# Convolved projection from its ninth row tile on, and the projection back, in two-by-two blocks with seven products

## The reference

```python
FFN_HIDDEN = 2816        # 22 tiles of 128
FFN_CONV = 3

def causal_depthwise_conv(x, w, b):
    xp = jnp.pad(x, ((0, 0), (k_width - 1, 0), (0, 0)))
    y = b
    for k in range(k_width):
        y = y + w[k] * xp[:, k:k + seq]
    return y

def conv_ffn(x, w_in, conv_w, conv_b, w_out):
    h = causal_depthwise_conv(x @ w_in, conv_w, conv_b)     # [1024, 5632]
    val, gate = jnp.split(h, 2, axis=-1)
    return (jax.nn.silu(gate) * val) @ w_out                # [1024, 1024]

f = conv_ffn(rms_norm(x, norm_ffn_g), ffn_w_in, ffn_conv_w, ffn_conv_b, ffn_w_out)
x = x + f
```

## Time and profile before

| | |
|---|---|
| median of 3 runs | 2450.54 us |
| span of the profiled execution | 2450.4 us |
| TensorE busy | 2352.4 us (96%) |
| VectorE / ScalarE / GpSimd busy | 1305.0 / 1205.5 / 919.7 us |
| TensorE, 1950 to 2400 us | busy 450.0 of 450 us |
| DMA, mean over the span | 78 GB/s |

### The profile page before, as it was taken

How to read it: one execution, slowest core, us unless ns; L and a number is a source line. 1 busy time by engine, 2 the same in 40 slices (tenths; PEclk the granted TensorE clock), 3 DMA queues, 4 the chain that set the end, 5 groups by cost and what they waited for, 6 DMA issues and landing times.

```text
span 2450.4 us, 35232 instructions
## 1 busy us (share of the span) xinstructions
PE 2352.4 (96%) x12078; PEld 1996.2 (81%) x12078; DVE 1305.0 (53%) x2729; ACT 1205.5 (49%) x2873; POOL 919.7 (38%) x1133
## 2 busy tenths in 40 slices
PE   7999999999999999999999998989899999999999
PEld 6888787878888878888888887877678888888887
DVE  7444667667885333356656565687866213322331
ACT  6444556656775444456656565555544213322331
POOL 5554322311245642221122223677765322322321
PEclk9999999999999999999999999999999999999999
DMA  6322101111243332322222235322223111111112
GB/s 220 112 70 65 39 23 31 35 29 50 65 135 98 97 120 72 95 76 81 82 90 83 85 92 161 117 82 87 74 85 96 57 43 52 50 50 48 49 52 85
DMA packets 305985, 191.87 MB, mean 78 GB/s; under 512 B 63760, under 2 KB 284176, under 8 KB 305296
## 3 DMA queue, kind: packets, MB, share of 16 engines
q1 hardware_dynamic: 305808, 189.61, 26.2%
HBM read 170.16 MB, written 19.40 MB: 77 GB/s over the span
## 4 chain that ended last, share of the span: by engine, by line
PE 82%; DVE 5%; ACT 4%; issue 4%; POOL 4%; DMA 1%; SPq 0%; POOLq 0%; DVEq 0%; ACTq 0%
PE PS L1544 21%; PE PS L1546 21%; PE PS L1545 21%; PE PS L1690 5%; PE PS L1657 5%; PE PS L1644 3%; PE PS L1645 2%; POOL WS L2375 2%; ACT PY L1775 1%; PE PS L1699 1%; POOL HT L2434 1%; POOL PT L2375 1%; PE PS L1599 1%; DVE EO L2227 1%; PE PS L1681 1%
## 5 line engine op out<-in xcount | busy, mean ns | idle before, releaser
L2375 POOL TENSOR_TENSOR WS<-WR,WS 128x256 fp32r<-128x256 f32 x773 | 595.0, 788 | 1206.1 <-ACT WS L1775 1205.4
L1544 PE MATMUL PS<-HT,WS 128*128 128x512 f32 x1760 | 709.4, 403 | 32.4 <-POOL HT L2434 10.1
L1546 PE MATMUL PS<-HT,WS 128*128 128x512 f32 x1760 | 690.7, 392 | 0.0
L1545 PE MATMUL PS<-HT,WS 128*128 128x512 f32 x1760 | 689.1, 392 | 0.0
L1775 ACT ACTIVATE WS<-WR 128x256 fp32r<-128x256 f32 x788 | 295.2, 409 | 259.0 <-PE PS L1546 221.2
L1544 PEld LDWEIGHTS PS<-HT,WS 128*128 128x128 f32 x1760 | 332.8, 189 | 102.6 <-issue 15.1
L1546 PEld LDWEIGHTS PS<-HT,WS 128*128 128x128 f32 x1760 | 332.5, 189 | 72.4
L1545 PEld LDWEIGHTS PS<-HT,WS 128*128 128x128 f32 x1760 | 333.6, 190 | 62.6
L1775 ACT ACTIVATE PT<-PS 128x512 fp32r<-128x512 f32 x352 | 185.9, 529 | 225.5 <-PE PS L1657 225.2
L2002 DVE TENSOR_TENSOR PT<-PS,PT 128x512 fp32r<-128x512 f32 x352 | 210.9, 609 | 68.5 <-ACT PT L1775 66.2
L1690 PE MATMUL PS<-PT,QKV 128*128 128x256 f32 (+1 forms) x1248 | 209.3, 289 | 3.2 <-DVE YB L2181 2.3
(11 more groups left out here) (195 smaller groups left out, 3702.2 us busy)
## 6 DMA issues: line engine op xcount, KB each, us to landing
WR<-in_ffn_in SPq DMA_DIRECT2D x120, 256.0 KB, 2.9
WR<-in_w_in_odd SPq DMA_DIRECT2D x106, 256.0 KB, 3.0
EO<-in_grid SPq DMA_DIRECT2D x48, 384.0 KB, 3.1
WR<-in_w_in_even SPq DMA_DIRECT2D x100, 128.0 KB, 2.5
WR<-in_w_out_odd SPq DMA_DIRECT2D x48, 256.0 KB, 2.9
yd<-PY SPq DMA_DIRECT2D x44, 256.0 KB, 3.3
WR<-in_w_in_even SPq DMA_DIRECT2D x34, 256.0 KB, 2.9
WR<-in_w_out_even SPq DMA_DIRECT2D x64, 128.0 KB, 2.8
```

Of the source, the lines that this page charges most:

```text
L1544: e.matmul(out, wh, rh, start=start, stop=False)
L1545: e.matmul(out, wh, rl, start=False, stop=False)
L1546: return e.matmul(out, wl, rh, start=False, stop=stop)
L2375: e.tensor_tensor(ws(i, 1, n), RAW[raw_slot(u)][:, o:o + n], f32(ws(i, 0, n)), ALU.subtract).then_inc(s_wlop.sem, 1)
```

## The change

The 28 tiles "in" from the ninth row tile on, and the whole projection back, are done as two-by-two block products with seven products of half size for eight. A `Quad` is one such product: for "in" the value and gate tile j (two block rows), the two halves of the 1024 input features, and the two halves of the tokens; for "out" two output tiles, even and odd hidden tiles, and the two halves of the tokens. Two quads (x = 0, 1) run interleaved as a unit: 7 units "in" (numbers 0 to 6 here), then 6 units "out", two for each of the groups of 4, 4 and 3 pairs of hidden tiles. A unit is 14 products of 12 matmuls (9 in the last two units). Products 0, 2, 4, 6 of a quad add up in one bank, 3 and 5 in another.

Both sides need sums: of weights (`s1` to `s4`, each 128x512, "weight sum", two by POOL, two by DVE), of the normed input (`turn_sums`, 32 DVE instructions of 128x512 and 16 splits during the n=1 passes), and of the hidden tiles (`pair_sums`). The seven moving blocks of each pair of hidden tiles are stored to a new DRAM tensor `ud` (77 blocks of 256 KB) and fetched and split again ("u load", "u split") during the unit before their group begins: 28 splits in unit 6, 28 in unit 8, 21 in unit 10. `X` is spilled to DRAM ("x spill", 8 x 512 KB), its tiles serve as room for the "in" units, and are fetched back ("x reload") when unit 7 begins. Weights are split 8 products ahead, now 512 columns at a time. After each product a "post" copies (ACT) or adds (DVE) the bank to a half tile; the product four later writes the same bank and waits for that post. The splits "half hi" and "half lo" are gone; the n=0 passes store their result instead.

```diff
+Y_BANKS, X_BANKS, Z_BANKS = ((1, 3), (5, 7)), (4, 6), (2, 0)
+GROUPS = ((0, 4), (8, 4), (16, 3))
+SPLIT_OF = (A11, A12, A11, ADD, A21, A12, A22)
...
+        def turn_sums():
+            for k in range(4):
+                ...
+                put("turn raws", k, tmp, base, free)
+                put("turn sums", tmp, base)
+                for z, (b, i) in enumerate(((2, 3), (3, 0), (4, 1), (6, 2))):
+                    put("turn split", tmp[i], b, k, base, hi, turned[b, k])
...
-                p.hi = s_fa.add()
-                put("half hi", p, n)
-                put("half lo", p, n)
+                if n == 0:
+                    put("u store", [HBUF[p.buf]], u.i, STORED_AT[b], d_h[p.buf], [(s_fd, p.product)])
...
+        def weigh(p):
+            p.before = [lambda: (s_gm, p.no - n + 1)]
+            on = (s_glv, s_glv, s_glp, s_glp, s_glv, s_glp, s_glp)[i]
+            put("weights", p)
...
+            for t, p in enumerate(run):
+                put("product", p)
+                if t:
+                    post(run[t - 1])
+                if t + n - 1 < len(run):
+                    weigh(run[t + n - 1])
+                ...
+                        if 0 <= b < 7 and z // 2 == z2 and z < GROUPS[g][1]:
+                            split_hidden(g, b, z, s0 - 14 + 2 * b + 2)
+                if 14 * entered - 4 <= t:
+                    bring_back(t)
...
+                elif kind == "product":
+                    w.wait_ge(s_gh, p.no + 1)
+                    w.wait_ge(*p.lo)
+                    w.wait_ge(*until[p.bank])
+                    for k in range(m.n):
+                        w.wait_ge(*p.ready[k])
+                        ...
+                        e.matmul(out, wh, rh, start=p.first and k == 0, stop=False, skip_group_check=True)
+                        e.matmul(out, wh, rl, start=False, stop=False, skip_group_check=True)
+                        last = e.matmul(out, wl, rh, start=False, stop=k == m.n - 1, skip_group_check=True)
+                    until[p.bank] = p.post
...
+                elif kind == "x spill":
+                    w.wait_ge(s_nd, ffn[1].nd[7])
+                    e.dma_start(d["xs"][c, :, :], X[:, c, :]).then_inc(d_xt[c].sem, 16)
+                elif kind == "x reload":
+                    e.dma_start(X[:, c, :], d["xs"][c, :, :]).then_inc(d_xt[c].sem, 16)
```

More of the change, by code:

```diff
@@ L1391, in odd_last @@
                     pool_task(1, (4, 6, 8, 9).index(i))
-            for i in range(16):
+            for i in range(2 * PLAIN):
                 half_task(i // 2, HID * (i % 2), 1)
[L1394 to L1418, removed]
@@ L1420, in enter_in @@
-        def enter_in(j, base, g0, g1):
-            plan.append(Ffn("in", j, base, g0, g1, *add_units(in_units(d["ffn_in"], [(base + 128 * j, 128)]))))
+        units_of = [[Quad("in", PLAIN + 2 * u + x, None, u, x) for x in (0, 1)] for u in range((HT_TILES - PLAIN) // 2)]
+        for group in GROUPS:
+            for v in range(2):
+                units_of.append([Quad("out", 4 * v + 2 * x, group, len(units_of), x) for x in (0, 1)])
+        quads = [m for unit in units_of for m in unit]
+        run = [Product(m, i, 0) for unit in units_of for i in range(7) for m in unit]
@@ new lines, in start_products, with open_products @@
+        def start_products():
+            early = [(s_mm, state["mm"]), (s_acc, s_acc.n), (s_sums, s_sums.n), (s_pp, blocks[1, 7].lo)] + ffn[1].lo
+            late_ = [turned[b, k] for b in (2, 3, 4, 6) for k in (2, 3)]
+            rooms.extend((r, early if r < 4 else late_ + early) for r in range(len(ROOM)))
+            urooms.append((3, late_ + early))
+            take_rooms()
+            state["opened"] = open_products
+        def open_products():
+            if not places and at["split"] == len(subs):
+                order = sorted(range(5), key=lambda k: max(split_after(k)))
+                places.extend([(k, split_after(k)) for k in order] + [(k, None) for k in range(5, 9)])
+            while places and state.setdefault("split", 0) < 5 and all(i in used for i in places[state["split"]][1]):
+                weigh(run[state["split"]])
+                state["split"] += 1
@@ new lines, in take_rooms, with sum_of @@
+        def take_rooms():
+            while rooms and wanted:
+                m, which = wanted.pop(0)
+                r, after = rooms.pop(0)
+                m.raw[which] = r
+                if which == ADD:
+                    m.landed[which] = after
+                else:
+                    m.landed[which] = [(d_room[r], d_room[r].add(16))]
+                    put("weight load", m, which, r, lambda after=after: after)
+        def sum_of(m, name, on, out, a, b, op, need):
+            m.sums[name] = (on, on.add())
+            cut = slice(0, 128 * m.n)
+            put("weight sum", on, ROOM[m.raw[out]][:, cut], ROOM[m.raw[a]][:, cut], ROOM[m.raw[b]][:, cut], op, need)
@@ new lines, in centre, with go, taps @@
+        def centre(m, c, t, col, need, at_, then):
+            def go():
+                mid = (s_ga, s_ga.add())
+                put("centre", m, c, t, col, need + list(x_at.get(t, ())), )
+                soon(at_ + 1, lambda: taps(mid))
+            def taps(mid):
+                at1 = s_gd.add()
+                done_ = (s_gd, s_gd.add())
+                put("taps", m, c, t, col, at1, mid)
+                if c == CV[m.x]:
+                    m.val = done_
+                else:
+                    m.gate = done_
+                then()
+            soon(at_, go)
```

620 lines of the change are left out of this document (470 added, 150 removed).

## The result

The changed kernel takes 2435.76 us (median of 4 runs, 2434.73 to 2439.86) where the kernel before, on the same chip, takes 2449.72 (4 runs, 2446.56 to 2451.54): a ratio of 0.9948, 95% interval 0.9934 to 0.9962. It is faster by 14.0 us and not by the 45 of the forecast, and it lies 1.8 us outside the range. The profiled execution took 2434.73 us, its span is 2432.9.

A forecast was written before the change was run, and what follows sets the result against it. TensorE was taken to bound the kernel, busy 2352.4 of 2450.4 us. The terms -67.9 + 2 + 14 + 1 - 2 + 3 + 4 = -45.9 gave 2405 us, own range 2392 to 2428, overall range 2384 to 2434.

The forecast's parts named there:

- Products, -67.9: Both projections: 300 matmuls fewer at an unchanged 0.2265 us each save 67.9 us.
- Units "in", +2: First six units: VectorE and GpSimd demand 33.2 of 38.05 us together and fit; 2 us lost, 0 to 15.
- Unit 6 itself: 28 hidden-block splits overload VectorE and GpSimd by 13.4 to 17.4 us; posts may lag 8.2, so TensorE waits 5 to 9.
- Unit 7, "about 5 us more show": X tiles fetched back land 5.0 to 8.2 us after their last taps; first posts wait, costing about 5 us more.
- Units 8 and 10, +1: Hidden splits in unit 8 make common demand even with the unit, 1 us (0 to 8); unit 10 nothing.
- n=0 passes, -2: Dropping "half lo" and eight ScalarE splits shortens the chain before the 6.4 us pooling wait: -2 us, -6 to 0.
- Spill, +3: n=1 passes: the 4.2 MB spill of X in SP's queue delays the next weights, 3 us, 0 to 12.
- Turning, +4 (0 to 10): n=1 passes: 40 added VectorE instructions put it 12 to 20 us behind; four banks allow 16.3; 4 us lost.
- Clock: After a TensorE wait of some 4 us or more, the low clock adds about 2 us; counted at units 6 and 7.
- all hidden: Rival, chance 0.18: unit 6's lag is absorbed, since only posts are tight; -67 us, 2383 us.
- Whole durations: Rival, chance 0.15: two-operand VectorE and GpSimd instructions never overlap; units "in" 1.1 over, unit 6 24.5 over; 2420 us.
- VectorE waits out every GpSimd instruction: Rival, chance 0.08: VectorE's queue waits so, TensorE follows it wherever both sums exceed the unit; slower, 2477 us.

The follow-up runs named there:

- e9: Changed kernel with all instructions of the turned input 16 columns wide instead of 512 and the X spill spread over eight steps: 2416.19 us, ratio 0.9863.
- e13: e1 with 15 of GpSimd's 17 instructions in unit 6 cut to 16 columns, VectorE's queue unchanged: 2415.98 us, ratio 0.9859.
- e1: Changed kernel with the fetches of X tiles 0 and 2 one step earlier, ahead of that step's hidden-block loads in SP's queue: 2429.77 us, ratio 0.9916.
- e8: Changed kernel with all instructions of the turned input 16 columns wide instead of 512: 2419.97 us, ratio 0.9876.
- e4: Changed kernel with the eight X spills issued one per piece of work, weight loads between them, instead of all at once: 2434.85 us, ratio 0.9939.
- e5: Changed kernel with early reload, turning spread over more of the n=1 passes and spill spread, all three together: 2413.27 us, ratio 0.9850.

## Why the prediction was wrong, point by point

- **Products, -67.9.** Right: 543.8 to 475.7 us is -68.1, at an unchanged pace. A unit takes 38.08 us where 38.05 was said.
- **Units "in", +2.** 0 us in units 1 to 5, and 4.4 in unit 0; in the range, but not for the reason given. TensorE's wait of 2.8 us in unit 0 ended with ScalarE's first post. That stood behind a silu of the last pass, which waited 4.95 us for VectorE's taps, and VectorE had low parts and sums of weights ahead of these, some at 1.78 us each. It isn't the lateness of the opening: in e9, where that is gone, unit 0 takes 42.6. I had no term for the change from passes to products.
- **Unit 6 itself.** 5 to 9 us of waits and 2 of clock were said; it has 7.3 us of waits and is 9.9 us long over 38.08. That VectorE and GpSimd hold each other up is the cause, as e13 shows, and the price of 0.44 us that a VectorE instruction takes out of GpSimd's time was good (1.70 - 1.295 = 0.41). But the count was wrong: of the 28 low parts only 15 of VectorE and 4 of GpSimd ran in unit 6, 6 and 3 in unit 7. With 27 + 8 instructions of VectorE and 18 of GpSimd, as e13 has them in the unit, the same sum gives 27 x 0.44 + 8 x 0.98 + 18 x 1.295 = 43 us (an estimate), 5 over, which the allowance of 8.2 would have covered. So the 7.3 us agree by luck. A mean over the unit is also too coarse, since the low parts stand in its later part; what that alone costs no run shows.
- **Unit 7, "about 5 us more show".** This step failed. It cost 21.5 us: waits of 16.7, the rest low clock behind them. I took the reload to start when its tile's last tap ends, and to be alone in SP's queue. I had not laid the queue of SP beside VectorE's: the reloads stood behind loads that wait for late low parts, and the second one's stood behind the very post that waited for the first reload. e1 undoes that for 8.5 us. And unit 7 inherits VectorE's lateness (another 5.8, e13), while 8.2 us of allowance had been used up in unit 6; I counted it for both. The 14 us of both units were 31.4.
- **Units 8 and 10, +1.** The size is right by luck: both take 38.08, and 1.4 us are lost in unit 9.
- **n=0 passes, -2.** The direction was right: the long wait is 2.6 us shorter, the whole part 4.8, within my range (-6 to 0). That the missing low parts are the reason fits, but no run tests it.
- **Spill, +3.** In range (0 to 12): 4.3 without the turning (e9 against e8), 5.0 with it, where e4 also starts the turning later. But the issue of eight stores took SP 8.15 us, where I had taken the 4.15 of eight loads.
- **Turning, +4 (0 to 10).** This term failed too: 17.2 (e8). I compared VectorE's delay (12 to 20 us) with the 16.3 us that four banks give. The wait did not come by VectorE's lateness alone: high parts of the turned input stand in ScalarE's queue ahead of weight splits and centre taps, and ScalarE stood 6.62, 3.82, 2.02 and 8.14 us before them. I named who waits for VectorE at the banks, and not who is queued behind the waiting instruction on ScalarE. With the spill spread, spreading the turning gives 8.0 us back (e4 to e5) and leaving it out 16.4 (e4 to e9), so about half of its cost is its place in the queues; how the rest divides between the engines' own work and ScalarE's waits no run shows.
- **Clock.** I gave it 2 us, once. The products' stretch is 37.2 us longer than its matmuls and its waits are 27.6, so about 10 us are low clock there; in the opening, waits grew by some 17 us and the stretch by 22.6, so about another 5. I had also priced only waits of some 4 us and more: behind those of 3.83, 3.27 and 2.76 us the mean granted clock of the next 5 us was 0.50, 0.66 and 0.71.

The sum by what was measured: -67.9 + 4.4 + 31.4 + 1.4 - 4.8 + 22.6 = -12.9, and with the 4.4 us from upstream -17.3, where the two spans differ by 17.5.

The rivals: "all hidden" is out. "Whole durations" had the better time (2420) for a wrong reason: it charged six units "in" 1.1 us each, and they have 0. "VectorE waits out every GpSimd instruction" has the price of one instruction right. In unit 6 a VectorE instruction with SBUF operands takes up to 1.78 us, its own 0.69 and most of GpSimd's 1.295. But it is paid in full only while both queues are full, so TensorE loses nothing in units 1 to 5: VectorE works about 32 us in each, 7 more than alone, and still rests.

The Trainium skill ("SBUF — State Buffer", section "SBUF: two separate sides") calls the shared port an exclusive lock for the whole instruction. Its turn-taking agrees with the rule. By whole durations a pair would take 0.688 + 1.295 = 1.98 us; the trace has 1.70. Only part of the 0.28 us between them is overlap of the two engines, since each engine's own instructions overlap a little as recorded: in a row they start 0.60 us apart on VectorE and 1.25 on GpSimd, 1.85 together. Where rule and trace differ the trace decides: a pair costs 1.70.

What stays open: in e13 unit 7 is still 7.1 us over. TensorE waits 4.8 us there, 1.9 for ScalarE's weight splits and the rest for posts; what is behind these wasn't tested. More rooms weren't tried.

## What to carry to other kernels

When a transfer is added, write down for each in-order queue what stands ahead of it and what that waits for, DMA queues too, and follow the circle until it closes: 8.5 us of unit 7 and about half of the turning's 17.2 lay in the order of the queues and not in the instructions' own time. Count what falls into a stretch from the order of the steps, and not from the number that belong to its work. Lateness allowed by buffers can be spent once; a unit that inherits it has none. And behind each new wait TensorE lost up to 2.4 us to the low clock beside the wait itself (12 matmuls at 0.43 us for 0.2265).

## What the runs showed of the hardware

- VectorE and GpSimd with SBUF operands of 128x512 and full queues take turns at 1.70 us a pair (0.69 and 1.295 alone, or 0.60 and 1.25 from start to start in a row). Posts, which read a bank, take 0.67 to 0.69 us all the same, in all 126 of the run.
- Of the two taps that VectorE makes in a row, now from SBUF, the first takes 1282 ns on average over units 1 to 5, as it did from a bank, and the second 1500, where from a bank it took 1282; beside GpSimd one took 2.20 us (at 2206, in unit 7).
- Eight stores of 512 KB kept SP busy for 8.15 us and landed in a median of 5.9 us; eight loads of that size took 4.15 and 8.2. Of the stores the first two took 0.46 and 0.42 us to issue, the last five 1.16 to 1.25 each.
